# A router's chain rebuilt: logits by token, a slot table from rank and expert one-hots, late biases

## The reference

```python
def hier_moe(x, wg, bg, we, be, w1, w3, w2):
    pg = softmax(xf @ wg + bg)
    g_sel = argmax(pg); p_top = pg[g_sel]
    le = (xf @ we + be).reshape(-1, N_GROUPS, EXPERTS_PER_GROUP)
    top_v, top_i = lax.top_k(le[g_sel], 2)
    pe = softmax(top_v)
    # y = sum over the two experts of p_top * pe * ((silu(x @ w1) * (x @ w3)) @ w2)
```

## Time and profile before

| | us |
|---|---|
| median of the runs (range) | 904.78 (904.13 to 905.32) |
| profiled execution, in all | 911.48 |
| its span, first to last instruction | 909.2 |
| PE busy | 795.3 (87%) |
| DVE busy | 352.5 (39%) |
| ACT busy | 169.7 (19%) |
| POOL busy | 119.1 (13%) |

### The profile page before, as it was taken

How to read it: one execution, slowest core, us unless ns; L and a number is a source line. 1 busy time by engine, 2 the same in 40 slices (tenths; PEclk the granted TensorE clock), 3 DMA queues, 4 the chain that set the end, 5 groups by cost and what they waited for, 6 DMA issues and landing times.

```text
span 909.2 us, 12840 instructions
## 1 busy us (share of the span) xinstructions
PE 795.3 (87%) x4940; PEld 469.6 (52%) x4940; DVE 352.5 (39%) x865; ACT 169.7 (19%) x357; POOL 119.1 (13%) x163
## 2 busy tenths in 40 slices
PE   7999999979998887887789999999899987788784
PEld 6745554765554444454277446447655534445451
DVE  2468986532111111111722789955311211111127
ACT  2304113101211111111211121221011111111113
POOL 0101030030111010011000000300211101011010
PEclk9999999989999999999979999999999999999997
DMA  9961933879999999997983038348799999999961
GB/s 291 306 243 60 317 98 88 279 220 353 419 416 416 414 416 414 416 416 275 340 267 138 1 125 245 97 122 321 233 392 415 415 418 415 416 416 416 392 232 53
DMA packets 107918, 266.57 MB, mean 293 GB/s; under 512 B 34775, under 2 KB 68587, under 8 KB 90902
## 3 DMA queue, kind: packets, MB, share of 16 engines
q1 hardware_dynamic: 97898, 254.11, 75.2%
q0 software_dynamic: 8640, 9.11, 2.9%
q10 hardware_dynamic: 1340, 2.80, 0.8%
HBM read 262.85 MB, written 25.92 MB: 318 GB/s over the span
## 4 chain that ended last, share of the span: by engine, by line
PE 52%; DMA 24%; issue 12%; DVE 6%; SPq 3%; ACT 1%; POOL 1%; DVEq 0%; POOLq 0%; ACTq 0%
DMA ring<-in_moe_w 22%; PE psum L1008 13%; PE psum L723 12%; PE psum L1034 9%; PE psum L702 7%; PE psum L654 3%; PE psum L734 2%; SPq L509 1%; DVE arena L1649 1%; DMA rows<-xn_scratch,sg 1%; PE psum L892 1%; PE psum L660 1%; SPq L505 1%; SPq L501 1%; PE psum L790 1%
## 5 line engine op out<-in xcount | busy, mean ns | idle before, releaser
L1008 PE MATMUL psum<-ring,arena 128*64 128x256 f32 x1984 | 229.2, 383 | 36.1 <-DVE arena L1649 26.0
L1008 PEld LDWEIGHTS psum<-ring,arena 128*64 128x64 f32 x1984 | 148.5, 137 | 102.2 <-issue 38.5
L1034 PE MATMUL psum<-ring,arena 128*64 128x512 f32 x496 | 124.9, 633 | 39.3 <-DMA ring<-in_moe_w 31.2
L1657 DVE SCALAR_TENSOR_TENSOR arena<-arena,psum 128x128 f32<-128x128 f32 x64 | 18.1, 282 | 298.7 <-ACT arena L1945 283.1
L723 PE MATMUL psum<-ring,uT 128*128 128x512 f32 x256 | 113.0, 595 | 0.0
L1034 PEld LDWEIGHTS psum<-ring,arena 128*64 128x64 f32 x496 | 40.3, 144 | 107.5 <-issue 106.2
L1649 DVE TENSOR_TENSOR arena<-psum,gff 128x512 f32<-128x512 f32 x64 | 41.2, 685 | 118.9 <-PE psum L654 118.9
L2063 POOL DMA_INDIRECT y_scratch<-arena,sg x28 | 28.3, 1010 | 374.8 <-ACT arena L1930 314.0
L723 PEld LDWEIGHTS psum<-ring,uT 128*128 128x128 f32 x256 | 47.7, 190 | 55.3 <-issue 54.5
L1935 ACT ACTIVATE arena<-psum 128x256 f32<-128x256 f32 x62 | 23.8, 384 | 280.1 <-PE psum L1008 270.8
L1930 ACT ACTIVATE arena<-psum,sg 128x512 f32<-128x512 f32 x64 | 44.0, 687 | 129.3 <-PE psum L1034 129.3
(11 more groups left out here) (285 smaller groups left out, 656.0 us busy)
## 6 DMA issues: line engine op xcount, KB each, us to landing
ring<-in_moe_w SPq DMA_DIRECT2D x186, 1024.0 KB
ring<-in_w_in SPq DMA_DIRECT2D x24, 1024.0 KB
ring<-in_w_out SPq DMA_DIRECT2D x8, 1024.0 KB
y_scratch<-sg SPq DMA_DIRECT2D x2, 2304.0 KB
ring<-y_scratch SPq DMA_DIRECT2D x4, 1024.0 KB, 9.8
arena<-in_state_ret SPq DMA_DIRECT2D x16, 128.0 KB, 6.2
out<-arena SPq DMA_DIRECT2D x16, 128.0 KB, 2.6
xn_scratch<-rows ACTq DMA_DIRECT2D x4, 512.0 KB, 4.6
```

The lines of the kernel that those rows point to most:

```text
L1008: i = pe.matmul(b[64 * j:64 * j + 64, 0:FE], xsT[:, u // 2, k, s], w[j][:, k, :], start=k == 0, stop=k == KT - 1, skip_group_check=True)
L1034: i = pe.matmul(b[64 * q:64 * q + 64, :], hT[:, q, f, :], w[:, 512 * j:512 * j + 512], start=f == 0, stop=f == 1, skip_group_check=True)
```

## The change

The logits are computed by token: `uT` is now the weights and `wr` streams, so each tile's result lies with tokens on partitions, 36 columns each, in banks `lg` (tiles 0 and 2) and `lgb` (tile 1). VectorE's `logit` multiplies by `rec` and adds the bias, held on all partitions, into `lgs`. `norm(l, 1, t)` transposes `x` itself; `rows` is made by ACT (`store_rows`) for the store to `xn_dram` only. The small tile's transposes stand ahead of `mixed(1, 1)`, logits of tile 0 behind it.

The table for the 32 experts' own blocks is made from `slot_oh` (one-hot over 64 slots of the pair's rank in its expert) and `tok_oh` (expert one-hot by token value), in two halves of the array for even and odd experts; a second one, `tabg`, from `gate_oh`, comes after `gidx`. What concerns overflow blocks (`overs`, 26 VectorE instructions; `table_over`; `overs_marked`) runs among the first experts. `gidx_ready` releases the gathers, `idx_ready` now comes after the overflow part. The load of `spare_w2` waits for it and stands behind the loads of `p == 4`. The filler counts change to 11, 5, 5 (new, `WAIT_GATES`) and 4. The bias loads move from ACT's first instructions to its place at L1811, as broadcasts to 128 partitions.

```diff
-WAIT_NORM, WAIT_CHOICE, WAIT_MARKS, WAIT_ROWS = (13, 8), 17, 26, 17
+WAIT_NORM, WAIT_CHOICE, WAIT_MARKS, WAIT_GATES, WAIT_ROWS = (13, 8), 11, 5, 5, 4
...
-    jobs += [("w2", 1), ("w10", 2), ("n2t0a", 3), ("n2t0b", 5), ("w11", 4), ("n2t2a", 6), ("lgT", 7),
-             ("n2t1a", 0), ("n2t1b", 3)]
-    jobs += [("lg", 2), ("cum", 5), ("tab", 6)]
+    jobs += [("w2", 1), ("w10", 2), ("n2t0a", 3), ("n2t0b", 5), ("n2t2a", 6), ("w11", 4), ("lg", 7),
+             ("n2t1a", 0), ("n2t1b", 3), ("lgb", 2)]
+    jobs += [("cum", 5), ("tab", 6), ("tabg", 7), ("tabo", 6)]
...
-                for i in range(2):
-                    sp.wait_ge(gath[i], 16 * (l * GROUPS + 1))
-                for f in range(2):
-                    sp.dma_start(spare_w2[f], w2[l, NE - 1, 128 * f:128 * f + 128, :]).then_inc(spare2_in, 16)
                 for p in range(2, NPAIR):
                     pair, it = pair_of(p)
                     a, b = 2 * pair, 2 * pair + 1
@@ -603,6 +603,10 @@
                     if 4 * it + b < NE - 1:
                         xfull(sp, "h", b, it - 1, l)
                         expert(l, it, b)
+                    if p == 4:
+                        sp.wait_ge(idx_ready, l + 1)
+                        for f in range(2):
+                            sp.dma_start(spare_w2[f], w2[l, NE - 1, 128 * f:128 * f + 128, :]).then_inc(spare2_in, 16)
                 xfull(sp, "y1", *pair_of(NPAIR - 3), l)
                 expert2(l, GROUPS - 1, 2)
 
...
@@ -665,8 +668,14 @@
                 if (s, t) == (0, 0):
 
                     keep_clock(psum[:, 3, :], WAIT_NORM[min(l, 1)])
-                pe.wait_ge(rows_ready, norm_turn(l, s, t))
-                r = rows[0:n, t % 2, :].rearrange("p (m k) -> p m k", k=KT)
+                if s:
+
+                    for name in ((f"w{t}0", f"w{t}1") if t < 2 else ("w2",)):
+                        freed(pe, l, name)
+                    r = x[0:n, t, :].rearrange("p (m k) -> p m k", k=KT)
+                else:
+                    pe.wait_ge(rows_ready, norm_turn(l, s, t))
+                    r = rows[0:n, t % 2, :].rearrange("p (m k) -> p m k", k=KT)
                 halves = (("a", 0, 4), ("b", 4, 8)) if t < 2 else (("a", 0, 8),)
                 for h, k0, k1 in halves:
...
 
-                def logits(o, n):
+                def logits(t):
+
+                    o, n = TILES[t]
+                    freed(pe, l, f"n2t{t}{'b' if t < 2 else 'a'}")
+                    b = bank("lg") if t == 2 else start(l, ("lg", "lgb")[t])
                     for k in range(KT):
-                        i = pe.matmul(bank("lgT")[0:NG + NE, o:o + n], wr[:, k, :], uTk[:, k, o:o + n], start=k == 0, stop=k == KT - 1)
-                    return i
+                        i = pe.matmul(b[0:n, 36 * t:36 * t + 36], uTk[:, k, o:o + n], wr[:, k, :], start=k == 0, stop=k == KT - 1,
+                                      skip_group_check=True)
+                    if t:
+                        done(i, ("lgb", "lg")[t - 1])
...
                 mixed(1, 1, (0, 1, 4, 5, 6, 7, 2, 3))
-                norm(l, 1, 2)
                 pe.wait_ge(wr_in, 32 * (l + 1))
-                freed(pe, l, "n2t0b")
-                start(l, "lgT")
-                logits(0, 128)
-                freed(pe, l, "n2t2a")
-                logits(SEQ, NT - SEQ)
+                logits(0)
                 norm(l, 1, 1)
...
-                freed(pe, l, "lgT")
-                b = start(l, "lg")[:, 0:3 * (NG + NE)].rearrange("p (t e) -> p t e", t=3)
-                for t, (o, n) in enumerate(TILES):
-                    i = transpose(b[0:n, t, :], lgT[:, o:o + n], NG + NE)
-                done(i, "lg")
+                logits(2)
+                logits(1)
 
                 b = start(l, "cum")
...
@@ -961,15 +967,33 @@
                 done(i, "cum")
 
 
-                b = start(l, "tab")
-                keep_clock(b, WAIT_MARKS)
-                b = b[:, 0:2 * NBLK]
-                for t, (o, n) in enumerate(TILES):
-                    pe.wait_ge(mark_ready, 3 * l + t + 1)
-                    pe.wait_ge(slot_marked, 3 * l + t + 1)
-                    for k in range(2):
-                        i = pe.matmul(b, slot_oh[0:n, t, k, :], blk_oh[0:n, t, k, :, :], start=(t, k) == (0, 0), stop=(t, k) == (2, 1))
-                done(i, "tab")
+                def table(b_, what):
+
+                    for h in range(2):
+                        b = b_[64 * h:64 * h + 64, 0:NPAIR]
+                        for t, (_, n) in enumerate(TILES):
+                            for k in range(2):
+                                i = pe.matmul(b, slot_oh[0:n, t, k, :], what[0:n, t, k, h:NE:2], start=(t, k) == (0, 0),
+                                              stop=(t, k) == (2, 1), skip_group_check=True)
+                    return i
+
+                def table_over():
+
+                    b = start(l, "tabo")[0:SLOTS, 0:2 * OVER]
+                    for t, (_, n) in enumerate(TILES):
+                        for k in range(2):
+                            i = pe.matmul(b, over_oh[0:n, t, k, :], blk_val[0:n, t, k, :, :], start=(t, k) == (0, 0),
+                                          stop=(t, k) == (2, 1), skip_group_check=True)
+                    done(i, "tabo")
+
+                keep_clock(start(l, "tab"), WAIT_MARKS)
+                pe.wait_ge(tok_marked, l + 1)
+                pe.wait_ge(slot_marked, l + 1)
+                done(table(bank("tab"), tok_oh), "tab")
+                start(l, "tabg")
+                keep_clock(bank("tabg"), WAIT_GATES)
+                pe.wait_ge(gate_marked, l + 1)
+                done(table(bank("tabg"), gate_oh), "tabg")
 
 
...
@@ -1076,6 +1100,8 @@
                 keep_clock(begin("x0", 0, 0), WAIT_ROWS)
                 tokens(0, 0)
                 experts2(0, 0, first=True)
+                pe.wait_ge(over_marked, l + 1)
+                table_over()
                 experts2(1, 0)
                 with pe.Fori(1, GROUPS - 1) as it:
                     experts2(0, it)
...
                 dve.wait_ge(rms_ready, norm_turn(l, s, t))
+                if s:
+                    dve.reciprocal(rec[0:n, t:t + 1], rms[0:n, t:t + 1]).then_inc(rec_ready, 1)
+                    return
                 do(dve.reciprocal(rec[0:n, t:t + 1], rms[0:n, t:t + 1]))
                 if t == 2:
 
                     full(dve, l, f"n{s + 1}t0b")
-                    if s:
-                        dve.wait_ge(xn_out[0], 16 * (l + 1))
                 S(rows[0:n, t % 2, :], x[0:n, t, :], rec[0:n, t:t + 1], None, ALU.mult).then_inc(rows_ready, 1)
 
             def turned(l, s, t):
...
@@ -1526,6 +1553,18 @@
                     s = x[:, t, 512 * h:512 * h + 512]
                     free(T(s, s, bank(name), ALU.add), name)
 
+                def logit(t):
+
+                    n = TILES[t][1]
+                    turn_ = 3 * l + (0, 2, 1)[t] + 1
+                    name = ("lg", "lgb", "lg")[t]
+                    full(dve, l, name)
+                    dve.wait_ge(rec_ready, turn_)
+                    if l == 0 and t == 0:
+                        dve.wait_ge(bias_in, 32)
+                    i = STT(lgs[0:n, t, :], bank(name)[0:n, 36 * t:36 * t + 36], rec[0:n, t:t + 1], lbias[0:n, l, :], ALU.mult, ALU.add)
+                    free(i, name) if t else own(i)
+
                 mixed(0, 0)
                 mixed(0, 1)
...
                 turned(l, 1, 0)
                 scaled(l, 1, 2)
+                turned(l, 1, 2)
                 mixed(1, 1)
-                turned(l, 1, 2)
+                turned(l, 1, 1)
                 scaled(l, 1, 1)
-                turned(l, 1, 1)
-
-
-                full(dve, l, "lg")
-                lg = bank("lg")[:, 0:3 * (NG + NE)].rearrange("p (t e) -> p t e", t=3)
-                G = lg[:, :, 0:NG]
+                logit(0)
+                logit(2)
+                logit(1)
+                freed(dve, l, "lgb")
+                freed(dve, l, "lg")
+                own.wait()
...
+                for k in range(2):
+                    i = T(tok_oh[:, :, k, :], onehot[:, :, k, :], bc(C("vals").rearrange("p (t k) -> p t k", k=2)[:, :, k].unsqueeze(2), [128, 3, NE]), ALU.mult)
+                    i.then_inc(tok_marked, 1) if k else own(i)
+
+                full(dve, l, "cum")
+                cum = bank("cum")[:, 0:128].rearrange("p (t e) -> p t e", t=4)
+                for k in range(2):
+                    own(T(rtmp[:, :, k, :], onehot[:, :, k, :], cum[:, 0:3, :], ALU.mult))
+                own.wait()
+                do(dve.tensor_reduce(rank[:, :, :], rtmp, AX, ALU.add))
+
+                def in_slots(out, place_):
+                    return T(out.rearrange("p t k s -> p (t k) s"), bc(C("iota")[:, 0:SLOTS].unsqueeze(1), [128, 6, SLOTS]),
+                             bc(place_.rearrange("p t k -> p (t k)").unsqueeze(2), [128, 6, SLOTS]), ALU.is_equal)
+
+                in_slots(slot_oh, rank).then_inc(slot_marked, 1)
+
```

(69 more changed lines are left out.)

142 lines of the change are left out of this document (62 added, 80 removed).

## The result

The new kernel takes 913.3 us (median of 5 runs, 910.9 to 914.8) where the kernel before takes 904.1 beside it: a ratio of 1.0099, 95% interval 1.0078 to 1.0119. I had forecast 901.9, with a range up to 908.0. The time is outside the range, and on the other side of no change. The rival in which the zeroing stands ahead of the gather had said 911.3. In the runs further down one execution of a_zs, which took 4409 us, is left out.

The account below looks back on a forecast made before the run. Bound: each expert phase is a fixed-length DMA weight stream whose start the router chain sets. Gather gains -10.7, clock +1.4, spare tile +5.0, overflow table +1.4 sum to -2.9 us: median 901.9, range 896.9 to 908.0.

Parts of the forecast that it names:

- The rival in which the zeroing stands ahead of the gather: Router: gathered rows complete only once the zeroing has drained, landing 3.5 us after it; +6.5 us, 911.3; chance 0.10.
- The gather's flight: Router, gather issue to rows: shares engines with the zeroing, 8.6 us in layer 0 and 7.5 in layer 1.
- 10.7 us forecast for logits, table and gather: Router: gather issued 7.65 us earlier per layer, less longer flights, gains 6.2 and 4.5 us, together 10.7.
- The clock: TensorE before layer 1's gathered rows: idle of about 3.5 us lowers the clock, charged 1.4 us, bounds 0 and 3.
- The table: Router, before `gidx`: 24 instructions at 44 ns each, 1.4 us plus 0.25 of tail.
- That rival (905.9): Tables slow: their 24 small instructions at 122 ns or at low clock, 2 us a layer, 905.9; chance 0.10.
- The spare tile: Expert weight stream: `spare_w2` moved behind pair 4's loads adds 2.5 us in each layer, 5.0 together.
- the overflow table: TensorE between the first two expert pairs: six calls, 12 instructions, charged 0.7 us per layer, 1.4 together.
- The start: Kernel start: bias loads leave it, but TensorE's filler runs on before the first norm, so nothing moves.
- the first VectorE step of the router: Router after the logits, layer 1: comes 1.2 us earlier, at 624.3, bounds 0.7 and 1.6.
- the store of tile 1: Router: issued some 3 us later, lands by 632.4, just ahead of the gather; being its last wait would show the forecast wrong.
- The base: Whole kernel: profiled run 6.7 us over the median of 904.78, a difference carried over from profiled 908.6 to median 901.9.

Follow-up runs that it names:

- a_zs: New kernel with y_scratch's zeroing issued ahead of group 0's last loads and the spare tile loaded right behind the first gathers; 0.9930 of the kernel before.
- a0: The new kernel unchanged, run again as the measure for its variants; 1.0079 of the kernel before.
- a_zero: New kernel with only the zeroing of y_scratch issued earlier, at 154.36 instead of 178.18 us in layer 0; 0.9964 of the kernel before.
- a_hz: New kernel with the zeroing cut in two halves, one issued early, one at its old place; 0.9931 of the kernel before.
- a_late: New kernel with the zeroing issued only when the first two gathers have landed, in front of the weight stream; 1.0013 of the kernel before.
- a_zsf: a_zs with more router filler, 17, 9, 9 and 16 rounds; 0.9882 of the kernel before.
- a_zsfn: a_zsf with four more rounds of filler ahead of the third tile's transposes at the start; 0.9858 of the kernel before.
- a_best: a_zsfn with the zeroing in two halves, early and at its old place, instead of whole; 892.6 us beside 906.4, 0.9853 of the kernel before.
- a_fill: New kernel with only more router filler, 17, 9, 9 and 26 rounds instead of 11, 5, 5 and 4; 1.0063 of the kernel before.
- a_spare: New kernel with the spare expert tile's halves loaded right behind the first gathers, the second half into tt; 1.0008 of the kernel before.
- b_bias: Kernel before with only the two bias loads moved behind the first stores in layer 0; 0.9994 of the kernel before.
- b_zero: Kernel before with only the zeroing of y_scratch issued about 23 us earlier; 1.0054 of the kernel before.
- a_actq: New kernel with the zeroing issued on ScalarE's queue at nearly the old time; 1.0054 of the kernel before.
- b0: The kernel before unchanged, for a second profiled execution; ratio 1.0014.
- b1: The kernel before unchanged once more, for a third profiled execution; ratio 0.9994.

## Why the prediction was wrong

The stages in the profiles, means of three of before and of two of the new kernel, us:

| stage | before | new | difference |
|---|---|---|---|
| start to the end of the last projection, layer 0 | 165.7 | 167.75 | +2.05 |
| to the first rows on TensorE | 30.2 | 27.1 | -3.1 |
| to the first expert load | 7.55 | 8.9 | +1.35 |
| to the end of the last projection, layer 1 | 411.4 | 414.7 | +3.3 |
| to the first rows | 28.05 | 24.45 | -3.6 |
| to the first expert load | 6.05 | 8.45 | +2.4 |
| to the end | 257.7 | 258.85 | +1.15 |
| sum | 906.65 | 910.2 | +3.55 |

**The gather's flight: the step that failed.** "I take 8.6 for layer 0 ... and 7.5 for layer 1", because the queue of GpSimd "shares, it does not line up behind". The flights were 10.7 and 7.4 (10.6 and 8.4 in a0). That layer 1's number is right is luck: its gather went out 2.7 us later than forecast (635.78 for 633.1), and its rows came 2.5 us later (643.14 for 640.6). The rows came when the zeroing was done, at 195.15 and 643.14; the rival had put them at 196.3 and 644.3. Of the 10.7 us forecast for logits, table and gather, 3.5 are there: rows 1 us earlier in layer 0 (2.05 less 3.1), 2.4 in layer 1 (1.2 for the small tile's transposes, less 3.6). The reading went wrong at the earlier trace rows: the 77 gather packets of 225 to 226 are of a gather under the weight stream, and I took them for what a gather does behind the zeroing. The row of the same two transfers, 193 to 194 in layer 0, showed the gather's packets flowing just as the zeroing ended, and I gave the rival 0.10 all the same. The rival's "3.5 us after the drain" was too long: in the new kernel the rows came 1.5 to 2 us behind it. a_zero, a_hz and a_late take the zeroing away from in front and the rows come 4.4 to 4.9 us sooner behind the last projection in layer 0, and 1.9 to 4.8 in layer 1. In the forecast's terms: -2.9, +7.2 for the rows, +2.35 for the clock (3.75 for 1.4) and -3.1 for the streams (3.3 for 6.4) make the ledger's +3.55.

**The clock: right kind, size too small.** I charged 1.4 us, to layer 1 alone. The rows to the first load took 1.35 and 2.4 longer, 3.75 together, since the low clock covers the transposes as well (1.97 for 1.16) and layer 0 too. There are two causes. The thinner filler lets the clock fall ahead of the table, and the transposes stay slow without the hold (1.97 in a_hz, 1.16 with more filler in a_zsf). The slow `up` is in layer 0 the hold's second bill: with an idle of 0.22 us before the rows (a_hz) it takes 3.67. But a_late and a_zs have a slow `up` in layer 1 (5.9 and 5.3) with no idle before the rows at all; only with no hold and more filler (a_zsf, a_zsfn, a_best) is it 3.67 in both layers.

**The table: mis-sized, and free.** 1.65 us forecast, tail included, 3.07 measured at 1.2 GHz and 1.84 to 1.87 at 2.4 GHz (a_zero, a_fill). The row that I chose, 44 ns each, was too low even for the full clock, where one takes 77. The filler ahead of it, also at 1.2 GHz, ran 0.5 and 0.9 us past VectorE's last mark and held the table back as long. a_fill shows that these losses cost nothing while the hold decided. That rival (905.9) was not the cause.

**The spare tile: right.** 2.5 us a layer forecast, 2 to 3.5 between the profiles with the tile late and early. But against the kernel before the stretches from the first load on grew by 2.1 (3.3 less the 1.2 of the moved transposes) and 1.15 only, not the 6.4 charged with the overflow table. In a_spare, with the tile early as in before, they are 0.7 and 1.3 us shorter than in before. The new kernel seems to win something back in its streams, but the three profiles of before differ by 4.2 us in the first of them; it isn't settled.

**The start.** Bias loads "at nothing": b_bias agrees (0.9994). In single executions the first group of matmuls starts 0.8 us earlier than in before, and then takes 8.03 us, as there, or 9.72 at a lower clock, so that it ends 0.6 us earlier (a_spare) or 0.9 later. Both profiles of the new kernel and that of b_bias have the slow one, and none of before's; in the new kernel's it is the 0.9 us of the ledger's first line beside the 1.2 of the transposes. I had let nothing move there. Here is that group in the new kernel, then in a_spare:

```profile
14.12 9.72 PE L711 MATMUL psum<-uT,ring 128*128 128x288 f32 x32 [0.52 <-DVE uT L1241]
```

```profile
14.11 8.03 PE L712 MATMUL psum<-uT,ring 128*128 128x288 f32 x32 [0.52 <-DVE uT L1242]
```

**Right:** the first VectorE step of the router 1.3 us earlier, counted from the start of `mixed(1, 0)`; the 26 instructions of `overs` hidden; the store of tile 1 never the gather's last wait; the overflow table 0.97 us.

**The base.** The ledger explains 3.55 of 7 to 9 us. Before's three profiled runs lie 6.7, 1.0 and -0.4 us from the medians beside them, 2.4 on average; the new kernel's -1.0 and 0.05, so -0.5. That is another 2.9. I "carried the difference over" of 6.7 as if it belonged to the kernel; it belonged to one execution. The last 1 to 3 us aren't accounted for.

## What to carry to other kernels

Before a transfer is issued earlier, list what is in flight at the new time, and price its landing by the drain of what is ahead, not by its own length: here the rows came when 2.3 MB of zeros had drained, and an issue 1 us earlier changed nothing. A bulk transfer that nobody waits for goes to where nothing small and urgent follows; check who else stands behind it there (the store in b_zero). And filler, clock and a shorter chain pay only once the wait that ends last is gone: a like filler gave 0.2%, within the scatter, with the hold and 0.5% without it.

## What the runs showed of the hardware

- A write of 2.3 MB from a small tile to DRAM moved 0.20 MB/us with the engines 95% busy, half of the weight stream's 416 GB/s at 100%, and a load on another queue, whose issue ended at 179.4, moved nothing until 187 (a_actq).
- The gather's flight without that traffic is 4.2 to 4.5 us (b_zero, and layer 1 of b0, b1 and b_bias; landing after 4.3 in layer 1 of a_zero). In layer 0 with the zeroing or half of it early, where the spare tiles, or they and half of the zeroing, are still in front, it is 6.4 to 8.3.
- TensorE's granted clock fell from 1.00 to 0.50 within 178 to 179, behind an idle of 1.47 us, and stayed at 0.50 until 202, though TensorE had work without a gap from 178.1 to 190.6 (new kernel); with more filler it was 1.00 from 168 to 188 (a_fill).
- 24 matmuls with 64 columns of weights and 16 streamed take 1.84 to 1.87 us at 2.4 GHz, 77 to 78 ns each, and 3.07 at 1.2 GHz, 128 ns.
- Executions of one kernel on one chip spread over 10 us (b1: 901.7 to 911.4 in 12 runs).
